# A two-block model on one core: small vectors moved to other queues, the first norm scaled by rows and turned by plain transposes, the first weight chunk split in halves

## The chip, the core and the metric

The kernel runs on one core of a Trainium2 chip, as one launch. The metric is the device time of that launch in microseconds (us), taken as the median of several executions. Everything is float32; large products are made of three fp32r products (below).

## The reference

Two transformer-like blocks follow one another on x of 256 tokens by 1024 features. Only the start matters here: the first layer of the first block is a Conformer convolution.

```python
def rmsnorm(x, g):
    xf = x.astype(jnp.float32)
    y = xf * lax.rsqrt(jnp.mean(xf * xf, axis=-1, keepdims=True) + EPS)
    return (y * g.astype(jnp.float32)).astype(x.dtype)

def conformer_conv(x, norm_g, pw1_w, pw1_b, dw_w, dw_b, ln_g, ln_b, pw2_w, pw2_b):
    a, b = jnp.split(rmsnorm(x, norm_g) @ pw1_w + pw1_b, 2, axis=-1)      # 1024 -> 2 x 1024
    h = a * jax.nn.sigmoid(b)
    h = lax.conv_general_dilated(h, dw_w[:, None, :], ...) + dw_b         # 31 causal taps, by channel
    h = jax.nn.silu(layernorm(h, ln_g, ln_b))
    return h @ pw2_w + pw2_b
```

What follows is a gated FFN, an attention with compressed, selected and windowed keys, a second FFN, a final norm, and then the second block (projections, mLSTM and forgetting attention, cross attention, an FFN, the last norm).

## The kernel before

**Work and buffers.** Every weight matrix is cut into chunks of up to 128 x 2048 values (1 MB). SP loads chunk c into `raw[c % 4]` (RAWS = 4) once the chunk four before it has been split; ScalarE (ACT) rounds it to `split_hi` (L579, a copy to fp32r), VectorE (DVE) writes the rest as `split_lo` (L944), and TensorE (PE) makes each product from three (L1469 to L1471). For five chunks of the start (numbers 3 and 6 of the first projection, and the first three of the second) GpSimd (POOL) writes `split_lo` instead (L544, list `by_pool`). There is no planner: each engine has its program written out in order, and semaphores join them. So an instruction that waits holds up all that stands behind it on its engine.

**The order of the start.** SP issues the two halves of x (`h`), chunk 0, five small vectors (L480), then the six loads of taps (L482: `taps` is 31 rows of 4 KB plus 4 rows of 4 KB, `pos` four small blocks), and then chunks 1, 2 and so on. ACT issues six small vectors (L572) and POOL three (L499). All 14 vectors lie as 128 rows in `vecs`; PE turns them at once (L1568) and DVE copies them to `vecT` (L986), from which gains and biases are then read as columns.

**The first norm.** ACT squares and sums each of the two token tiles (L597), POOL makes the reciprocal root (L506, L509), ACT puts it on a diagonal (`root_diag`, L592), and PE multiplies x by that diagonal, which turns and scales it in one step (`turn`, L1484: 16 products of 128 x 128, each of them two MATMULs in the trace). ACT writes the high half `xn_hi` of the turned, gained values (`take_hi`, L617, four pairs), DVE the low half `xn_lo` (`take`, L963).

**The first projection and the convolution.** `pw1` has eight chunks, one for each feature tile ft. For ft = 0 PE goes through the eight slices kt of the input as `xn_lo` comes; after ft = 0 it turns the taps (`turn_taps`, L1576 and L1579, which wait for `taps_loaded`), and then goes on with ft = 1 to 7. For every ft, ACT first splits chunks up to ft + 2, then takes the sigmoid (L647), and builds diagonals of taps (L637) after DVE has copied the taps (L1004, L1007); DVE splits up to ft + 2, then makes the gated value `u` (L996). After ft = 1, DVE starts its share of the 31 taps (L1025 for the first, L1028 for the others), with the remaining splits and gates put in after every four taps. PE does the other channels' taps (L1599).

Of the kernel before, what the change touches and what calls it, by code (L numbers as in the profile page):

```python
# [67 lines left out]
def build_kernel(nc, a, out):  # L68
# [8 lines left out]
    with ctx:  # L77
# [121 lines left out]
        vecs_loaded_pool = sem("vecs_loaded_pool")  # L199
        vecs_loaded_sp = sem("vecs_loaded_sp")  # L200
        small_loaded = sem("small_loaded")
# [256 lines left out]
        for b, name in enumerate(("cmp_pos_k", "cmp_pos_v")):  # L458
            for g in range(2):
                tap_loads.append((pos[:, P * b + DH * g:P * b + DH * g + DH], a[name]))  # L460
        pool_loads, act_loads, sp_loads = vec_loads[0:3], vec_loads[3:9], vec_loads[9:]


        @block.sync
        def _(sp):
# [3 lines left out]
            for c, parts in enumerate(chunks):  # L469
                if c >= RAWS:  # L470
                    last = c - RAWS
                    if is_split[last]:
                        sp.wait_ge(*lo_count(last))
                    else:
                        sp.wait_ge(*freed[last])
                for place, src in parts:
                    sp.dma_start(place(raw[c % RAWS]), src).then_inc(raw_loaded[c % RAWS], 16)  # L477
                if c == 0:
                    for dst, src in sp_loads:
                        sp.dma_start(dst, src).then_inc(vecs_loaded_sp, 16)  # L480
                    for dst, src in tap_loads:
                        sp.dma_start(dst, src).then_inc(taps_loaded, 16)  # L482
# [87 lines left out]
        def _(sc):  # L570
            for dst, src in act_loads:
                sc.dma_start(dst, src).then_inc(vecs_loaded, 16)  # L572
            def split(c, m):

                sc.wait_ge(raw_loaded[c % RAWS], loads_through(c))
                if m >= SPLITS:
                    sc.wait_ge(*freed[of_split[m - SPLITS]])
                n = used_cols[c]
                nc.scalar.activation(split_slot[m % SPLITS][0][:, 0:n], raw[c % RAWS][:, 0:n],  # L579
                                     ACT.Copy).then_inc(split_hi, 1)  # L580

            through = splitter(split)

            def squares(k, src, ready, together=False):

                idx = turning.index(k) if k in turning else None

                def diagonal(t):
                    if idx:
                        sc.wait_ge(turned, 4 * idx)  # L590
                    sc.wait_ge(rstd_ready, TT * k + t + 1)
# [3 lines left out]
                for t in range(TT):  # L595
                    ready(t)
                    nc.scalar.activation(scaled[:, t, :], src[:, t, :], ACT.Square, scale=D ** -0.5,  # L597
                                         accum_out=ssq[:, TT * k + t:TT * k + t + 1]).then_inc(ss_ready, 1)
                    if idx is not None and not together:
                        diagonal(t)  # L600
                for t in range(TT if together else 0):
                    diagonal(t)

# [4 lines left out]

            def take_hi(k, which=0):

                name, off = gains[k][which]
                for n in range(4):
                    if which == 0:
# [319 lines left out]
        def _(ve):  # L933
# [12 lines left out]
            def split(c, m):  # L946
# [3 lines left out]
                ve.wait_ge(split_hi, m + 1)  # L950
                n, (hi, lo) = used_cols[c], split_slot[m % SPLITS]
                less_hi(lo[:, 0:n], raw[c % RAWS][:, 0:n], hi[:, 0:n]).then_inc(split_lo, 1)

            through = splitter(split)

            def take(k, which=0):

                name, off = gains[k][which]
                for n in range(4):
                    ve.wait_ge(xn_hi, xn_before[k] + 4 * which + n + 1)  # L960
# [486 lines left out]
        def _(te):  # L1447
# [4 lines left out]
            def weights(stage, n, k, unsplit=False):  # L1452
# [7 lines left out]
                te.wait_ge(*lo_count(c))  # L1460
                return c, [kn(s, used_cols[c] // k, k) for s in split_slot[nth[c] % SPLITS]]
# [16 lines left out]
            def turn(k, src=h):  # L1478

                idx = turning.index(k)  # L1480
                for t in range(TT):
                    te.wait_ge(root_diag_ready, TT * idx + t + 1)
                    for kt in range(KT):
                        x = mm(bank[kt // 2][:, S * (kt % 2) + P * t:S * (kt % 2) + P * t + P],  # L1484
                               src[:, t, P * kt:P * kt + P], root_diag[:, t, :], start=True, stop=True)
                        if t == TT - 1 and kt % 2:
                            x.then_inc(turned, 1)

            def features(dst, w, c0, ready=None):
# [18 lines left out]
            def feature_pair(stage, n, b, before=None, ready=None):  # L1508
# [4 lines left out]
                for j in range(2):  # L1513
                    x = features(bank[b][:, S * j:S * j + S], w, P * j, ready if j == 0 else None)
                used(c, x)
# [50 lines left out]
            te.wait_ge(vecs_loaded_pool, 16 * len(pool_loads))  # L1566
            te.wait_ge(vecs_loaded_sp, 16 * len(sp_loads))
            nc.tensor.transpose(bank[4][:, 0:P], vecs, ident[:, :]).then_inc(pre_turned, 1)  # L1568
# [373 lines left out]
```

## Time and profile before

| | |
|---|---|
| median of 3 runs | 1200.13 us (1198.3 to 1204.06) |
| the profiled execution | 1200.32 us, its span 1198.5 us |
| busy of the span: PE, PEld, DVE, ACT, POOL | 94%, 83%, 56%, 46%, 8% |
| first 31.7 us: PE, DVE, ACT busy | 20.3, 12.4, 18.6 us |
| 31.7 to 120.5 us: PE, DVE, POOL busy | 77.5, 88.8, 25.0 us |
| mean granted PE clock | 0.956 of full |

PE is TensorE's products and PEld its weight loads, which overlap them. The span runs from the first instruction to the last; the profiled execution was 1.8 us longer than its span. The time of a stage is not read from the busy shares but from what the engine that ends the stage waited for. In the rows, times are microseconds from the start of the span; "x8" is the number of instructions merged into a line; the bracket at the end of a line is the idle time before it and what ended it; "SPq" and "ACTq" are the queues in which SP and ACT issue transfers.

### The profile page before, as it was taken

What the parts mean: (1) busy time and instruction counts of PE and PEld (TensorE: products, weight loads), DVE (VectorE), ACT (ScalarE), POOL (GpSimd) and SP (SyncE); (2) the same over time, 40 slices, a digit from 0 to 9 for tenths busy, and PEclk for the clock granted to TensorE, in tenths of its full rate; (3) what the DMA queues carried; (4) which work ended last, traced back from release to release, by engine and by line L of the source; (5) the groups of instructions that cost most, each with busy time, mean ns of one, the idle gap of its engine ahead of it and who ended that gap; (6) DMA issues with size and microseconds to landing.
All of it is one profiled execution on the core that took longest, in us unless ns stands there. A gap on an engine that the chain in (4) does not pass through costs nothing.

```text
span 1198.5 us, 17458 instructions
## 1 busy us (share of the span) xinstructions
PE 1122.6 (94%) x7303; PEld 996.4 (83%) x7303; DVE 674.5 (56%) x1099; ACT 549.7 (46%) x888; POOL 92.2 (8%) x107
## 2 busy tenths in 40 slices
PE   6996699999999988899999979999999999999997
PEld 6985479999989955689999979999756888999996
DVE  3999545455455379555544547546424445555554
ACT  5760344444443478454444345535423444444442
POOL 3440056000010000000000010000000000000000
PEclk9998699999999889899999989999958999999999
DMA  8650045666582600546667554554402424655640
GB/s 234 197 150 1 3 139 176 195 183 185 177 182 71 236 11 1 171 137 197 182 177 207 178 159 140 168 186 141 141 1 71 141 72 145 205 177 176 209 142 35
DMA packets 188312, 170.74 MB, mean 142 GB/s; under 512 B 15398, under 2 KB 164006, under 8 KB 188234
## 3 DMA queue, kind: packets, MB, share of 16 engines
q1 hardware_dynamic: 187128, 167.20, 45.8%
q10 hardware_dynamic: 1010, 2.43, 0.6%
q8 instruction: 57, 0.93, 0.3%
q14 instruction: 21, 0.17, 0.0%
q0 software_dynamic: 96, 0.02, 0.0%
HBM read 168.58 MB, written 1.05 MB: 142 GB/s over the span
## 4 chain that ended last, share of the span: by engine, by line
PE 79%; DVE 14%; ACT 3%; POOL 1%; SPq 1%; issue 1%; DMA 1%; POOLq 0%; ACTq 0%; DVEq 0%
PE bank L1469 23%; PE bank L1470 23%; PE bank L1471 23%; DVE v L1028 6%; PE bank L1484 1%; PE bank L1818 1%; PE bank L1817 1%; ACT scaled L597 1%; DVE soft L1165 1%; DVE split_lo L944 1%; DVE soft L1146 1%; PE bank L1645 1%; SPq L477 1%; PE bank L1841 1%; POOL msq L506 1%
## 5 line engine op out<-in xcount | busy, mean ns | idle before, releaser
L944 DVE TENSOR_TENSOR split_lo<-raw,split_hi 128x2048 fp32r<-128x2048 f32 (+1 forms) x152 | 344.5, 2268 | 244.5 <-ACT split_hi L579 244.5
L1469 PE MATMUL bank<-xn_hi,split_hi 128*128 128x256 f32 x1440 | 410.9, 285 | 3.7 <-DVE xn_lo L963 3.6
L1470 PE MATMUL bank<-xn_lo,split_hi 128*128 128x256 f32 x1440 | 408.4, 284 | 0.0
L1471 PE MATMUL bank<-xn_hi,split_lo 128*128 128x256 f32 x1440 | 408.3, 284 | 0.0
L579 ACT ACTIVATE split_hi<-raw 128x2048 fp32r<-128x2048 f32 (+1 forms) x157 | 296.5, 1890 | 151.3 <-PE bank L1471 145.2
L1469 PEld LDWEIGHTS bank<-xn_hi,split_hi 128*128 128x128 f32 x1440 | 277.1, 192 | 7.6 <-issue 5.5
L1470 PEld LDWEIGHTS bank<-xn_lo,split_hi 128*128 128x128 f32 x1440 | 277.2, 193 | 1.3
L1471 PEld LDWEIGHTS bank<-xn_hi,split_lo 128*128 128x128 f32 x1440 | 277.2, 192 | 0.0
L1469 PE MATMUL bank<-split_hi,ffa_hi 128*128 128x512 f32 x304 | 118.7, 390 | 0.0
L1470 PE MATMUL bank<-split_lo,ffa_hi 128*128 128x512 f32 x304 | 118.7, 390 | 0.0
L1471 PE MATMUL bank<-split_hi,ffa_lo 128*128 128x512 f32 x304 | 118.3, 389 | 0.0
L1469 PE MATMUL bank<-split_hi,xn_hi 128*128 128x512 f32 (+3 forms) x256 | 96.5, 377 | 5.1 <-DVE xn_lo L944 5.1
L1470 PE MATMUL bank<-split_lo,xn_hi 128*128 128x512 f32 (+3 forms) x256 | 95.4, 373 | 0.0
L1471 PE MATMUL bank<-split_hi,xn_lo 128*128 128x512 f32 (+3 forms) x256 | 95.3, 373 | 0.0
L695 ACT ACTIVATE soft<-bank 128x256 f32<-128x256 f32 x44 | 16.9, 385 | 137.0 <-PE bank L1471 137.0
L1028 DVE SCALAR_TENSOR_TENSOR v<-u,tapT,v 128x256 f32<-128x256 f32 x147 | 75.3, 580 | 0.0
L506 POOL TENSOR_SCALAR msq<-ssq 128x1 f32<-128x1 f32 x20 | 10.6, 528 | 755.8 <-ACT scaled L597 755.5
L1471 PEld LDWEIGHTS bank<-split_hi,ffa_lo 128*128 128x128 f32 x304 | 57.1, 188 | 12.0
L1469 PEld LDWEIGHTS bank<-split_hi,ffa_hi 128*128 128x128 f32 x304 | 57.2, 188 | 11.0
L1470 PEld LDWEIGHTS bank<-split_lo,ffa_hi 128*128 128x128 f32 x304 | 57.2, 188 | 10.6
L1469 PEld LDWEIGHTS bank<-split_hi,xn_hi 128*128 128x128 f32 x256 | 49.8, 194 | 17.5 <-DVE xn_lo L944 5.0
L1471 PEld LDWEIGHTS bank<-split_hi,xn_lo 128*128 128x128 f32 x256 | 49.7, 194 | 8.4
(256 smaller groups left out, 1103.2 us busy)
## 6 DMA issues: line engine op xcount, KB each, us to landing
raw<-in_ffn_w_in SPq DMA_DIRECT2D x88, 512.0 KB, 5.2
raw<-in_w_ff SPq DMA_DIRECT2D x32, 1024.0 KB, 5.1
raw<-in_ffn_w_out SPq DMA_DIRECT2D x22, 1024.0 KB, 4.8
raw<-in_w_in SPq DMA_DIRECT2D x14, 1024.0 KB, 5.5
raw<-in_a_pw_w SPq DMA_DIRECT2D x16, 512.0 KB, 6.9
raw<-in_w_xkv SPq DMA_DIRECT2D x8, 1024.0 KB, 5.3
raw<-in_a_pw_w SPq DMA_DIRECT2D x4, 1024.0 KB, 5.4
raw<-in_b_w_in SPq DMA_DIRECT2D x4, 1024.0 KB, 6.1
```

What stands on the lines that cost most here:

```text
L477: sp.dma_start(place(raw[c % RAWS]), src).then_inc(raw_loaded[c % RAWS], 16)
L506: nc.gpsimd.tensor_scalar(msq[:, c:c + 1], ssq[:, c:c + 1], EPS, None, ALU.add).then_inc(ms_ready, 1)
L579: nc.scalar.activation(split_slot[m % SPLITS][0][:, 0:n], raw[c % RAWS][:, 0:n], ACT.Copy).then_inc(split_hi, 1)
L597: nc.scalar.activation(scaled[:, t, :], src[:, t, :], ACT.Square, scale=D ** -0.5, accum_out=ssq[:, TT * k + t:TT * k + t + 1]).then_inc(s ...
L695: nc.scalar.activation(softf[:, b], bank[ft % 4][:, 0:S], ACT.Silu).then_inc(gate_act, 1)
L944: return nc.vector.tensor_tensor(dst, src, hi.bitcast(F32), ALU.subtract)
L1028: x = nc.vector.scalar_tensor_tensor(out=dst, in0=src, scalar=tap, in1=dst, op0=ALU.mult, op1=ALU.add)
L1146: x = nc.vector.tensor_tensor_reduce(out=scores_of(i)[:, piece], in0=src, in1=bias, scale=-DH ** -0.5, scalar=3e38, op0=ALU.add, op1=ALU.m ...
L1165: x = nc.vector.tensor_scalar(scores_of(i)[:, piece], scores_of(i)[:, piece], coef[:, i % 2, n:n + 1], None, ALU.mult)
L1469: mm(dst, left[0], right[0], start=start, stop=False)
L1470: mm(dst, left[0], right[1], start=False, stop=False)
L1471: return mm(dst, left[1], right[0], start=False, stop=stop)
```

## The change

The five small vectors leave SP: ACT now issues the first twelve of the 14, POOL the last two. The six loads of taps go behind chunk 3 instead of behind chunk 0. The first norm no longer builds diagonals on ACT: DVE multiplies the rows of each token tile by their reciprocal root into `scaled`, and PE turns `scaled` with 16 plain transposes. Chunk 0 is split in two halves of 1024 columns: ACT writes the first high half, then the first two pairs of `xn_hi`, then the second half, then the other two pairs; DVE does the same with the low halves; PE starts ft = 0 after the first low half and waits for the second at kt = 4. All other norms keep their diagonals.

```diff
-        pool_loads, act_loads, sp_loads = vec_loads[0:3], vec_loads[3:9], vec_loads[9:]
+        pool_loads, act_loads = vec_loads[12:], vec_loads[0:12]
...
-                if c == 0:
-                    for dst, src in sp_loads:
-                        sp.dma_start(dst, src).then_inc(vecs_loaded_sp, 16)
+                if c == RAWS - 1:
                     for dst, src in tap_loads:
                         sp.dma_start(dst, src).then_inc(taps_loaded, 16)
...
-                n = used_cols[c]
-                nc.scalar.activation(split_slot[m % SPLITS][0][:, 0:n], raw[c % RAWS][:, 0:n],
+                n, done = used_cols[c], 0
+                if c == 0:
+                    done = SLOT // 2
+                    nc.scalar.activation(split_slot[0][0][:, 0:done], raw[0][:, 0:done],
+                                         ACT.Copy).then_inc(first_hi, 1)
+                    sc.wait_ge(pre_copied, 1)
+                    take_hi(CONV, ns=range(2))
+                nc.scalar.activation(split_slot[m % SPLITS][0][:, done:n], raw[c % RAWS][:, done:n],
                                      ACT.Copy).then_inc(split_hi, 1)
...
-            squares(CONV, h, lambda t: sc.wait_ge(x_loaded[t], 16), together=True)
+            squares(CONV, h, lambda t: sc.wait_ge(x_loaded[t], 16))
             through(0)
-            sc.wait_ge(pre_copied, 1)
-            take_hi(CONV)
+            take_hi(CONV, ns=range(2, 4))
...
             ve.wait_ge(pre_copied, 1)
+            for t in range(TT):
+                ve.wait_ge(rstd_ready, t + 1)
+                nc.vector.tensor_scalar(scaled[:, t, :], h[:, t, :], rstd[:, t:t + 1], None,
+                                        ALU.mult).then_inc(x_scaled, 1)
+            ve.wait_ge(first_hi, 1)
+            half = slice(0, SLOT // 2)
+            less_hi(split_slot[0][1][:, half], raw[0][:, half], split_slot[0][0][:, half]).then_inc(first_lo, 1)
+            take(CONV, ns=range(2))
             through(0)
-            take(CONV)
+            take(CONV, ns=range(2, 4))
...
-                    te.wait_ge(root_diag_ready, TT * idx + t + 1)
+                    te.wait_ge(*((root_diag_ready, TT * (idx - 1) + t + 1) if idx else (x_scaled, t + 1)))
                     for kt in range(KT):
...
+                        if idx:
+                            x = mm(dst, src[:, t, P * kt:P * kt + P], root_diag[:, t, :], start=True, stop=True)
+                        else:
+                            x = nc.tensor.transpose(dst, scaled[:, t, P * kt:P * kt + P], ident[:, :])
...
                 for kt in range(KT):
+                    if rest and kt == KT // 2:
+                        te.wait_ge(*rest)
```

## Rows read from the trace of the kernel before

**Rows 1.** The page's chain of work that ended last, shares of the span.
```profile
PE 79%; DVE 14%; ACT 3%; POOL 1%; SPq 1%; issue 1%; DMA 1%; POOLq 0%; ACTq 0%; DVEq 0%
```

**Rows 2.** The same chain in order of time, start: start us, us, what.
```profile
16.04 6.69 DMA raw<-in_a_pw_w
...
22.75 1.92 ACT split_hi L579
...
31.09 0.49 DVE u L996
```

**Rows 3.** The timeline of the first 24.5 us: start us, us, engine, line, operation.
```profile
2.79 0.35 ACTq L572 DMA_DIRECT2D pt<-in_final_norm  x1
...
4.54 1.28 ACT L597 ACT_TABLE_LOAD   x1 [4.54 <-DMA h<-in_x]
...
8.41 0.58 POOL L509 TENSOR_TENSOR rstd<-msq,nhalf 128x1 f32<-128x1 f32 x1
...
10.82 0.45 PE L1568 MATMUL bank<-ident,pt 128*128 128x128 f32 x1 [10.82 <-DMA pt<-in_ln]
...
15.63 3.03 ACT L617 ACTIVATE xn_hi<-bank,vecT 128x256 fp32r<-128x256 f32 x8 [4.18 <-PE bank L1484]
...
17.53 0.36 PE L1469 MATMUL bank<-xn_hi,split_hi 128*128 128x256 f32 x1 [0.61 <-DVE xn_lo L963]
...
23.57 0.69 PE L1576 MATMUL bank<-ident,v 35*128 35x35 f32 x8
```

**Rows 4.** Transfer packets by size, of 9.0 to 15.5 and of 15.5 to 16.9 us.
```profile
DMA packets 2134, 1.14 MB, mean 176 GB/s; under 512 B 202, under 2 KB 2099, under 8 KB 2134
...
DMA packets 143, 0.07 MB, mean 48 GB/s; under 512 B 16, under 2 KB 143, under 8 KB 143
```

**Rows 5.** Stretches: start:end, length; last: PE clock, mean share of 16 transfer engines, GB/s.
```profile
16.00:16.50 0.50, 0.50 (x7) 0.50 (x6) 0.00 (x0) 0.50 (x3) 0.00 (x0) 1.00 0.08 23
...
26.00:30.00 4.00, 4.00 (x35) 4.00 (x35) 1.87 (x4) 2.55 (x5) 0.00 (x0) 1.00 1.15 293
```

**Rows 6.** Transfers by line: count, KB each, median us from issue to landing.
```profile
out<-scaled SPq DMA_DIRECT2D x2, 512.0 KB, 2.6
...
pt<-in_a_norm POOLq DMA_DIRECT2D x1, 4.0 KB, 5.8
```

**Rows 7.** DVE's instruction groups by shape: count, busy us, mean ns, idle before.
```profile
L944 DVE TENSOR_TENSOR split_lo<-raw,split_hi 128x2048 fp32r<-128x2048 f32 x150 | 343.7, 2293 | 242.6 <-ACT split_hi L579 242.6
...
L1165 DVE TENSOR_SCALAR soft<-soft,coef 128x256 f32<-128x256 f32 x24 | 7.3, 346 | 0.0
...
L1165 DVE TENSOR_SCALAR soft<-soft,coef 128x128 f32<-128x128 f32 x24 | 5.7, 280 | 0.0
```

**Rows 8.** PE: the first turn (min/median/max ns), and eight plain transposes later on.
```profile
L1484 PE MATMUL bank<-root_diag,h x32: 274/421/421, 11.1 to 16.6; 128*128 128x128 f32 x32
...
911.17 0.86 PEld L1857 LDWEIGHTS bank<-ident,u 128*128 128x128 f32 x8 [0.17 <-issue]
```

**Rows 9.** The timeline of POOL and DVE during the taps, 30 to 57 us.
```profile
30.78 4.63 POOL L544 TENSOR_TENSOR split_lo<-raw,split_hi 128x2048 fp32r<-128x2048 f32 x1 [15.76 <-ACT split_hi L579]
...
46.69 6.80 POOL L544 TENSOR_TENSOR split_lo<-raw,split_hi 128x2048 fp32r<-128x2048 f32 x1 [11.28 <-ACT split_hi L579]
...
31.68 4.21 DVE L1025 TENSOR_SCALAR v<-u,tapT,vecT 128x256 f32<-128x256 f32 x2
...
45.75 3.24 DVE L1028 SCALAR_TENSOR_TENSOR v<-u,tapT,v 128x256 f32<-128x256 f32 x8
...
49.31 7.23 DVE L1028 SCALAR_TENSOR_TENSOR v<-u,tapT,v 128x256 f32<-128x256 f32 x8
```

**Rows 10.** Stretches later: length; busy us of PE, PEld, DVE, ACT, POOL; PE clock.
```profile
31.70:120.50 88.80, 77.46 (x481) 71.42 (x480) 88.80 (x162) 43.88 (x107) 25.03 (x5) 0.95 0.38 112
...
110.00:112.00 2.00, 0.00 (x0) 0.00 (x0) 2.00 (x6) 0.00 (x0) 0.00 (x0) 0.77 0.00 0
...
433.00:436.00 3.00, 3.00 (x17) 1.41 (x14) 1.39 (x7) 2.01 (x10) 0.00 (x0) 0.50 0.00 0
```

More of the change, by code:

```diff
@@ L199, in build_kernel @@
         vecs_loaded_pool = sem("vecs_loaded_pool")
-        vecs_loaded_sp = sem("vecs_loaded_sp")
+        first_hi = sem("first_hi")
+        first_lo = sem("first_lo")
+        x_scaled = sem("x_scaled")
         small_loaded = sem("small_loaded")
@@ L577, in split, with squares @@
                     sc.wait_ge(*freed[of_split[m - SPLITS]])
-                n = used_cols[c]
-                nc.scalar.activation(split_slot[m % SPLITS][0][:, 0:n], raw[c % RAWS][:, 0:n],
+                n, done = used_cols[c], 0
[6 more added lines that the diff above has]
+                nc.scalar.activation(split_slot[m % SPLITS][0][:, done:n], raw[c % RAWS][:, done:n],
                                      ACT.Copy).then_inc(split_hi, 1)
             through = splitter(split)
-            def squares(k, src, ready, together=False):
+            def squares(k, src, ready):
                 idx = turning.index(k) if k in turning else None
                 def diagonal(t):
-                    if idx:
-                        sc.wait_ge(turned, 4 * idx)
+                    sc.wait_ge(turned, 4 * idx)
                     sc.wait_ge(rstd_ready, TT * k + t + 1)
@@ L598, in squares @@
                                          accum_out=ssq[:, TT * k + t:TT * k + t + 1]).then_inc(ss_ready, 1)
-                    if idx is not None and not together:
+                    if idx:
                         diagonal(t)
-                for t in range(TT if together else 0):
-                    diagonal(t)
             def h_squares(k):
@@ L607, in h_squares, with take_hi @@
                 squares(k, h, lambda t: sc.wait_ge(h_ready, h_count(k, t)))
-            def take_hi(k, which=0):
+            def take_hi(k, which=0, ns=range(4)):
                 name, off = gains[k][which]
-                for n in range(4):
+                for n in ns:
                     if which == 0:
@@ L951, in split, with take @@
                 n, (hi, lo) = used_cols[c], split_slot[m % SPLITS]
+                if c == 0:
+                    less_hi(lo[:, n // 2:n], raw[0][:, n // 2:n], hi[:, n // 2:n]).then_inc(split_lo, 1)
+                    return
                 less_hi(lo[:, 0:n], raw[c % RAWS][:, 0:n], hi[:, 0:n]).then_inc(split_lo, 1)
             through = splitter(split)
-            def take(k, which=0):
+            def take(k, which=0, ns=range(4)):
                 name, off = gains[k][which]
-                for n in range(4):
+                for n in ns:
                     ve.wait_ge(xn_hi, xn_before[k] + 4 * which + n + 1)
@@ L1459, in weights @@
                     return c, raw[c % RAWS]
-                te.wait_ge(*lo_count(c))
+                te.wait_ge(*((first_lo, 1) if c == 0 else lo_count(c)))
                 return c, [kn(s, used_cols[c] // k, k) for s in split_slot[nth[c] % SPLITS]]
@@ L1513, in feature_pair @@
                 for j in range(2):
-                    x = features(bank[b][:, S * j:S * j + S], w, P * j, ready if j == 0 else None)
+                    x = features(bank[b][:, S * j:S * j + S], w, P * j, ready if j == 0 else None,
+                                 lo_count(0) if c == j == 0 else None)
                 used(c, x)
```

7 lines of the change are left out of this document (3 added, 4 removed).

## The prediction

> **What bounds the kernel now.** I read the page's chain of waits first. It is TensorE for 79% and DVE for 14% [rows 1]; in the stretch from 31.7 to 120.5 us DVE is busy for all of its 88.8 us, PE for 77.5 [rows 10]. So two things can end the start: DVE's convolution taps, which follow on its second gated value at 31.09 us [rows 2], and PE's eight feature tiles, which feed them. Whatever the change brings has to show as an earlier start of that stretch; behind it everything runs relative to it. The whole start before the taps is 31 us, and 0.5% of the kernel, about what a measurement of it can tell from no change, is 6.0 us. That alone makes a large result unlikely.
>
> Then I followed what leads to 31.09. The chain in order of time goes from chunk 2's transfer, issued at 16.04 and landed 6.69 us later, over its split on ACT at 22.75 and DVE's half of it to the gated values [rows 2]. PE's own line runs beside it: the vectors land at 10.82, ACT begins `take_hi` at 15.63 after 4.18 us of idling, PE begins ft = 0 at 17.53, turns the taps at 23.57, and goes on with ft = 1 behind them [rows 3]. ft = 0 took 5.9 us, to 23.4; ft = 1, begun near 24.4 behind 0.9 us of turning, ends near 30.3, and with ACT's sigmoid of 0.5 us behind it that is 0.3 us ahead of 31.09. Both lines are therefore nearly critical, and the later of the two decides after the change.
>
> **The vectors.** ACT's six loads end at 3.14, each 0.35 us [rows 3]; six more make it 5.2. x landed at 4.54 [rows 3], so the squares start 0.7 us later, and the second reciprocal root, which was done at 8.99 [rows 3], comes at 9.65. For the landing of the last vector the nearest rows are 2.6 us (an unhurried store) and 5.8 us (POOL's vector among the same traffic) [rows 6]: 7.8 to 11.0 us. I take 9.2, nearer to the loaded row's middle. The last one landed at 10.82 before. PE turns them in 0.45 us [rows 3], and with 0.3 for DVE's copy `vecT` stands at 10.0 in place of 11.6.
>
> **The scaling.** A DVE multiply by a column costs 280 ns at 128 columns and 346 at 256 [rows 7], 66 ns per 128, so 742 ns at 1024: two take 1.5 us, with 0.3 for POOL, which builds masks then. The first tile is ready at 10.9, the second at 11.8. ACT saves its two diagonals (off the path now, since it idles 4.18 us behind them [rows 3]).
>
> **The transposes.** The old turn is 32 MATMULs, mostly at 421 ns and at 274 in the end [rows 8], from 11.06; ACT got its first pair after about 20 of them, 4.5 us. Now PE makes 16, and the first pair needs ten. Eight plain ones took 0.86 us at full rate [rows 8]; double that for an engine just out of idling, 0.2 each: 2.0 us. ACT begins `take_hi` at about 13.0 instead of 15.63, 2.6 us earlier.
>
> **The halves.** The first chunk was split at no cost before, while ACT and DVE had nothing else to do. The first half still is free. The second (0.95 us on ACT, half of 1.92 [rows 2], and 1.15 us on DVE, half of 2.29 [rows 7]) now stands between the second and the third pair of `xn`. From 15.63 to PE's first product were 1.9 us [rows 3], so PE starts at 14.9; it would want kt = 4 at 16.4, but ACT writes two pairs to 14.5, the half to 15.5, the third pair to 16.2, and DVE its half to 16.7 and the third pair to 17.6. PE waits 1.2 us there, and ends ft = 0 at 22.2 against 23.4. So of the 2.6 us the halving gives back 1.2 to 1.4. As far as PE's line goes, the change is worth 1.2 us, with the vectors at their bounds 2.6 or a loss of 0.6.
>
> **The taps' loads.** This is what I expect to decide. They were behind chunk 0 on SP's queue and are now behind chunk 3, and PE must turn them between ft = 0 and ft = 1. Between 9.0 and 15.5 us exactly 35 packets of 2 KB and more went through, none after that [rows 4]: these are the 31 + 4 rows of 4 KB of `taps`, so they took 6 us and more, about one row in 0.18 us. At 16.0 to 16.5 the 16 transfer engines were busy for 0.08 at 23 GB/s [rows 5]: a single engine, still behind with its share of chunk 1, with the other 15 out of work. The rows of taps thus go one behind the other through one engine, at some 21 GB/s. That also explains chunk 1's late landing before, and it means that moving the loads frees chunks 1 to 3: at 293 GB/s [rows 5] a chunk takes 3.6 us, and with chunk 0 through at 9.0, where the large packets began, they land near 12.5, 16 and 19.5 (on that one engine 64 KB at 20 GB/s are 3.3 us, so its third share ends at 18.9); ACT and DVE no longer wait for chunks 1 and 2. But the taps start at 18.9, need 5.4 us (their 124 KB at 23 GB/s) to 6.4, and a landing adds about 0.9: they are there at 25.2 to 26.2, I take 25.7. PE ended ft = 0 at 22.2: it idles 3.5 us, turns the taps till 26.6, and starts ft = 1 2.2 us later than the 24.4 of before.
>
> The Trainium skill says why one engine: in "DMA: Bandwidth & Descriptors", section "Why a DMA increments its semaphore by 16 and not by 1", a hardware-issued transfer runs on the largest count up to 16 that divides its slowest dimension on both sides, and 31 rows leave 1. The packets of [rows 4] agree with it; by the page's 27 GiB/s for an engine 124 KB would be 4.4 us, an estimate that would land the taps near 24.2.
>
> **From there to the taps' arithmetic.** `tapT` is copied by 26.9, ACT's first diagonals end at 28.1 and chunk 3's high half at 30.0, POOL's low half runs 30.0 to 34.6 (4.63 us [rows 9]). The sigmoid of ft = 1 waits for PE until 32.5, `u` is there at 33.4 instead of 31.5. And yet DVE loses nothing by that: its first two taps, of a shape that costs 0.35 us each [rows 7], took 4.21 us before, the first until 35.6, just to the end of POOL's 30.78 to 35.41, and eight taps took 7.23 us instead of 3.24 beside POOL's next one [rows 9]. DVE's taps and POOL's subtraction exclude each other. After the change DVE idles through most of POOL's piece, and is through its first tap at about 34.9 against 35.56. Its later gates wait for PE's tiles, 2.1 us later than before: 1.5 us for the fifth tile's, in part while POOL runs anyway. I put the end of the taps between 0 and 1.6 us later, and take 0.8.
>
> **The sum.** +0.7 (ACT's issue) is inside the 9.65 and hidden behind the vectors; PE line -1.2, taps' landing +3.4 on PE, together +2.2 at ft = 1; of these, 1.4 is swallowed by POOL's piece: +0.8. The profiled execution of 1200.32 would be 1201.1, the median of 1200.13 gives 1200.9. Behind 120.5 no instruction changes, only the phase of PE's clock, for which I have no price but the 1.5 us to either side that the three runs lie apart.
>
> **Rivals.**
> The taps are in time (landed by 22.2: the engine's rows go faster than 18.8 + 3.4, or turn out to be spread). Then PE's line counts, -1.2, and POOL's piece, starting before DVE is ready, adds up to 2 us: 1196.9 to 1199, about 1197.8. For it: nothing in the old trace waits for the taps, so their landing is never seen; against: the 35 packets in 6 us.
>
> PE's clock. With PE idle its granted clock fell from full towards half within 110 to 112 [rows 10], and at the start it took most of the first turn's 5.9 us until MATMULs came down from 421 to 274 ns [rows 8]. An idle stretch of 3.5 us ahead of ft = 1 can do the same: some 4 us of work at half rate cost 2 us more on PE, and DVE's gates follow: +2.5 to +4, 1203.4. The Trainium skill, "TensorE: Matmul & The Clock Gate", section "Part 4: PE-mode transpose", states that transposes do not count as work for the clock; if so, the first norm no longer warms PE for ft = 0, which by the half rate above would cost up to 2 us there, mostly hidden by the wait for the taps. The trace does not contradict: at 433 to 436, among attention's transposes, PE is busy throughout at clock 0.50 [rows 10].
>
> Slower than the measure can miss: the same wait for the taps, if the landing is at 31.5 us or later (each us later than 26 is a full us on PE and, past POOL's piece, on DVE). It would take the taps' engine another 5 us, as if chunk 4's traffic slowed it to half. The median would be 1206 and more. Against it: the taps shared the engines with chunk 1 before, and took 6.4 us.
>
> The change does not do what it says, since the vectors still land near 11 us: PE's ft = 0 ends at 24.0, still before the taps: the time is the same as in the forecast.
>
> **How the numbers follow.** Taps late, with the forecast's small loss (vectors late or not): 0.50. Taps in time: 0.31, of which 0.04 reach 1194.1. Clock: 0.14, of which 0.01 reaches 1206.1. Taps very late: 0.05. That is 0.04 faster by over 0.5%, 0.90 within, 0.06 slower. The range reaches over the case of taps in time and that of the clock, 1196.5 to 1204.5; the likeliest case's own is 1199 to 1203.
>
> **What would show it.** Right: the 35 large packets lie at about 19 to 25 us, PE's L1576 starts near 25.7 with an idle stretch of some 3 us ended by a transfer; `take_hi` starts at 13.0, PE's first product at 14.9, with a gap of about 1 us at kt = 4; chunk 2 is split without a wait for its transfer; POOL's L544 starts near 30 while DVE idles, and the first L1025 ends near 35. Wrong: L1576 directly behind ft = 0 (rival one), MATMULs of ft = 1 mostly at the slow duration (rival two). The step that I trust least is the landing of the taps, then how DVE, POOL and PE share the next 40 us.

## The result and the profile after

The changed kernel takes 1205.8 us (median of 9 runs, 1204.63 to 1207.61), the kernel before 1200.33 beside it (9 runs, 1198.3 to 1204.06): ratio 1.0045, 95% interval 1.0032 to 1.0058. That is 5.5 us slower, outside the range of the prediction (1196.5 to 1204.5) and 0.45% where the prediction had set the line of a slower kernel at 0.5%.

| | before | after |
|---|---|---|
| span of the profiled execution | 1198.5 | 1204.1 us |
| vectors landed (PE turns them) | 10.82 | 10.95 |
| first `take_hi` on ACT | 15.63 | 15.06 |
| PE's first product of ft = 0 | 17.53 | 16.95 |
| PE done with ft = 0 (end of its last product) | 23.64 | 24.98 |
| PE turns the taps | 23.57 | 28.11 |
| end of DVE's taps (start of the line that adds PE's) | 120.49 | 125.76 |

The last line is the measure that I use below: up to it the taps are 5.27 us late, and the span is 5.6 us longer. So the loss is made in the start and only carried from there. It also is a sharper measure than the total time, as the section on the experiments shows.

The page's chain of the kernel after, shares of the span, answers to [rows 1]: PE has 2% more, DVE 2% and ACT 1% less.

```profile
PE 81%; DVE 12%; ACT 2%; SPq 1%; POOL 1%; issue 1%; DMA 1%; POOLq 0%; ACTq 0%; DVEq 0%
```

The same chain in order of time, for [rows 2]. It no longer goes through chunk 2, its split and the gated value, but through the last of the taps' loads and then PE:

```profile
15.49 1.69 SPq L482
17.23 0.79 SPq L482
...
19.34 8.72 DMA pt<-in_cmp_pos_v
28.11 1.06 PE bank L1594 x8
...
29.52 0.51 PE bank L1482
30.03 0.21 PE bank L1483
...
35.48 0.12 PE bank L1483
```

Two things are to be seen. The transfer issued at 19.34 is complete 8.72 us later, and PE's products behind it are 0.21 us apart until 35 us, 0.12 from there on. The timeline of the start, for [rows 3]:

```profile
5.31 0.33 ACTq L572 DMA_DIRECT2D pt<-in_ln_x  x1
5.73 1.28 ACT L602 ACT_TABLE_LOAD   x1 [5.73 <-issue]
...
9.60 0.58 POOL L509 TENSOR_TENSOR rstd<-msq,nhalf 128x1 f32<-128x1 f32 x1
...
10.95 0.45 PE L1586 MATMUL bank<-ident,pt 128*128 128x128 f32 x1 [10.95 <-DMA pt<-in_ln_x]
...
11.76 1.45 DVE L995 TENSOR_SCALAR scaled<-h,rstd 128x1024 f32<-128x1024 f32 x2
...
12.56 3.67 PE L1501 MATMUL bank<-ident,scaled 128*128 128x128 f32 x16 [1.17 <-DVE scaled L995]
...
15.06 1.57 ACT L620 ACTIVATE xn_hi<-bank,vecT 128x256 fp32r<-128x256 f32 x4 [4.07 <-PE bank L1501]
...
16.95 0.55 PE L1482 MATMUL bank<-xn_hi,split_hi 128*128 128x256 f32 x1 [0.71 <-DVE xn_lo L968]
...
18.87 3.76 ACT L585 ACTIVATE split_hi<-raw 128x2048 fp32r<-128x2048 f32 x2
...
28.11 1.06 PE L1594 MATMUL bank<-ident,v 35*128 35x35 f32 x8 [3.13 <-DMA pt<-in_cmp_pos_v]
```

The twelve vectors on ACT's queue are issued by 5.64 and land at 10.95: nothing is won on the 10.82 of before. Chunks 1 and 2 are split back to back (18.87, no idle time ahead), so they do come earlier. And PE idles 3.13 us for the taps. The granted clock of the stretches around that wait (length; busy us of PE, PEld, DVE, ACT, POOL; clock; share of the transfer engines; GB/s), for [rows 10]:

```profile
25.00:27.00 2.00, 0.00 (x0) 0.00 (x0) 0.84 (x2) 0.47 (x1) 0.00 (x0) 1.00 0.74 217
27.00:29.00 2.00, 0.90 (x8) 0.90 (x8) 0.00 (x0) 0.00 (x0) 0.00 (x0) 0.78 0.38 110
29.00:31.00 2.00, 2.00 (x11) 1.86 (x11) 0.58 (x2) 1.18 (x4) 0.00 (x0) 0.50 0.80 222
31.00:33.00 2.00, 2.00 (x11) 2.00 (x11) 0.00 (x0) 1.60 (x1) 0.31 (x1) 0.50 0.91 268
33.00:35.00 2.00, 2.00 (x12) 2.00 (x11) 0.00 (x0) 0.00 (x0) 2.00 (x1) 0.51 1.09 314
35.00:37.00 2.00, 2.00 (x19) 2.00 (x19) 0.00 (x0) 0.00 (x0) 2.00 (x1) 1.00 0.62 174
```

PE is busy throughout from 29 on, with 11 products in 2 us at clock 0.50 (the 1.2 GHz level) and 19 at 1.00 (2.4 GHz). ft = 1 takes from 29.5 to 37.6 us, 8.2 instead of 5.9 of before. The packets of the stretches 16 to 20 and 20 to 28 us, for [rows 4], show where the taps were:

```profile
DMA packets 2176, 1.08 MB, mean 270 GB/s; under 512 B 90, under 2 KB 2175, under 8 KB 2176
...
DMA packets 2203, 1.18 MB, mean 148 GB/s; under 512 B 178, under 2 KB 2169, under 8 KB 2203
```

One large packet before 20 us and 34 from there to 28, with the mean rate down to 148 GB/s from 270. The beginning of the taps on DVE and POOL, for [rows 9]:

```profile
32.69 4.58 POOL L544 TENSOR_TENSOR split_lo<-raw,split_hi 128x2048 fp32r<-128x2048 f32 x1 [16.73 <-ACT split_hi L585]
...
38.42 0.48 DVE L1009 SCALAR_TENSOR_TENSOR u<-bank,vecT,soft 128x256 f32<-128x256 f32 x1 [8.63 <-ACT soft L649]
39.00 0.74 DVE L1038 TENSOR_SCALAR v<-u,tapT,vecT 128x256 f32<-128x256 f32 x2
...
125.76 0.42 DVE L1052 TENSOR_TENSOR v<-v,bank 128x256 f32<-128x256 f32 x1
```

POOL's piece is over at 37.27, before DVE has its gated value, and the first two taps take 0.74 us in place of 4.21.

### The profile page after: what moved, and what is told of

Read it like the earlier page. It is cut to its first block, busy times and chain, and to the rows that moved or that the text cites. A ratio compares the mean times of both kernels' runs of the same rounds, so it can differ in the third digit from the quotient of the medians.

```text
span 1204.1 us, 17428 instructions
## 1 busy us (share of the span) xinstructions
PE 1125.5 (93%) x7287; PEld 998.8 (83%) x7287; DVE 671.9 (56%) x1102; ACT 548.8 (46%) x887; POOL 88.9 (7%) x106
## 4 chain that ended last, share of the span: by engine, by line
PE 81%; DVE 12%; ACT 2%; SPq 1%; POOL 1%; issue 1%; DMA 1%; POOLq 0%; ACTq 0%; DVEq 0%
PE bank L1482 24%; PE bank L1483 24%; PE bank L1484 24%; DVE v L1041 5%; PE bank L1499 1%; PE bank L1836 1%; PE bank L1835 1%; SPq L479 1%; ACT scaled L602 1%; DVE soft L1178 1%; DVE soft L1159 1%; DMA pt<-in_cmp_pos_v 1%; PE bank L1663 1%; PE bank L1859 1%; POOL msq L506 1%
## 5 line engine op out<-in xcount | busy, mean ns | idle before, releaser
L585 ACT ACTIVATE split_hi<-raw 128x2048 fp32r<-128x2048 f32 (+2 forms) x157 | 295.6, 1885 | 147.9 <-PE bank L1484 145.4
L697 ACT ACTIVATE soft<-bank 128x256 f32<-128x256 f32 x44 | 16.9, 385 | 137.0 <-PE bank L1484 137.0
```

The source lines that it names most:

```text
L585: nc.scalar.activation(split_slot[m % SPLITS][0][:, done:n], raw[c % RAWS][:, done:n], ACT.Copy).then_inc(split_hi, 1)
L697: nc.scalar.activation(softf[:, b], bank[ft % 4][:, 0:S], ACT.Silu).then_inc(gate_act, 1)
```

## The experiments

All of them in one table. "Taps' end" is the start of DVE's L1039 of before, under whatever line number; "rest" is the span less that time; "clock" is PE's granted clock in 420 to 500 us, in attention.

| run | median us | ratio to before, 95% | first product | taps turned | taps' end | rest | clock |
|---|---|---|---|---|---|---|---|
| before | 1200.33 | | 17.53 | 23.57 | 120.49 | 1078.0 | 0.91 |
| after | 1205.8 | 1.0045 (1.0032 to 1.0058) | 16.95 | 28.11 | 125.76 | 1078.3 | 0.91 |
| e1_taps_back | 1201.73 | 1.0016 (0.9997 to 1.0034) | 17.60 | 24.89 | 120.52 | 1075.9 | 0.94 |
| e2_taps_only | 1205.6 | 1.0051 (1.0033 to 1.0070) | 17.46 | 28.02 | 124.65 | 1081.5 | 0.89 |
| e3_taps_16_15 | 1200.43 | 0.9998 (0.9978 to 1.0018) | 17.12 | 24.40 | 119.13 | 1081.4 | 0.87 |
| e4_fill | 1202.2 | 1.0019 (0.9999 to 1.0040) | 16.91 | 27.97 | 122.70 | 1073.9 | 0.94 |
| e5_no_halves | 1200.11 | 0.9997 (0.9981 to 1.0014) | 16.77 | 23.14 | 117.89 | 1080.9 | 0.91 |
| e6_before_16_15 | 1196.72 | 0.9988 (0.9970 to 1.0005) | 17.14 | 23.17 | 118.14 | 1075.7 | 0.94 |
| e7_sp_vecs_first | 1199.91 | 1.0003 (0.9986 to 1.0020) | 16.41 | 23.83 | 118.59 | 1079.5 | 0.87 |
| e8_diag_vecs_first | 1200.87 | 1.0011 (0.9995 to 1.0027) | 16.26 | 23.58 | 118.33 | 1080.8 | 0.91 |
| e9_combined | 1197.82 | 0.9987 (0.9972 to 1.0001) | 15.09 | 22.27 | 117.53 | 1076.0 | 0.94 |
| e10_vecs_only | 1200.92 | 1.0003 (0.9988 to 1.0017) | 17.50 | 23.54 | 120.35 | 1078.8 | 0.87 |
| e11_scaling_only | 1200.49 | 1.0004 (0.9989 to 1.0019) | 17.59 | 25.65 | 120.40 | 1078.0 | 0.91 |
| e12_before_16_15_again | 1198.93 | 0.9999 (0.9980 to 1.0017) | 17.49 | 23.54 | 118.43 | 1075.8 | 0.94 |

The column "rest" covers code that no edit touches, and yet lies between 1073.9 and 1081.5. The five profiles with 1076.0 and less are the five with that clock at 0.94; all others have 0.91 or less. So a start that is 2 us shorter can't be read from one total, and hardly from a median. The taps' end tells it better (118.14 and 118.43 for e6 and e12, which are the same kernel), but each run has one profile, and PE's clock within the start moves that end too: by 1 to 2 us in after, e7 and e11, as said at each.

### e1: the taps' loads back behind chunk 0

```diff
-                if c == RAWS - 1:
+                if c == 0:
                     for dst, src in tap_loads:
```

> The changed kernel with one edit undone: the loads of the taps stand behind chunk 0 again. If their late landing is the loss (PE idle 3.1 us before the taps, ft = 1 begun at 29.5 instead of 24.4 and at half clock until 34.9), PE turns the taps directly behind ft = 0, ft = 1 begins near 25.8 at full clock, and the time falls by 4 to 6 us against the changed kernel, to 1200 to 1202. If the vectors, the halves or the plain transposes are the loss, at least 3 of the 5.5 us stay: 1203.5 or more.

PE turned the taps without a wait at 24.89 and the taps' end came back to 120.52, all of the loss. ACT, by its line of chunk 2, waits for the chunks again, as before:

```profile
22.79 1.92 ACT L585 ACTIVATE split_hi<-raw 128x2048 fp32r<-128x2048 f32 x1 [1.19 <-DMA raw<-in_a_pw_w]
```

The move of the loads is what costs; the other parts together are worth nothing (120.52 against 120.49).

### e2: that move alone, in the kernel before

```diff
                         sp.dma_start(dst, src).then_inc(vecs_loaded_sp, 16)
+                if c == RAWS - 1:
                     for dst, src in tap_loads:
```

> The kernel before with one edit: the loads of the taps go behind chunk 3. If the taps' landing is the loss, PE ends ft = 0 near 23.4 and still waits until about 28, and the time is 1204.5 to 1206.5, the whole of the loss from this edit alone. If the rest of the change carries the loss, it stays within 2 us of 1200.3.

In the median it makes the whole loss by itself (ratio 1.0051), and PE waits as in this line:

```profile
28.02 1.06 PE L1577 MATMUL bank<-ident,v 35*128 35x35 f32 x8 [4.45 <-DMA pt<-in_cmp_pos_v]
```

At the taps' end it makes 4.2 of the 5.3 us (124.65 against 125.76 of after). The taps landed at the same time, so the missing 1.1 us are not theirs. The granted clock stood at half by 27 us already, while PE idled (0.50 in 27 to 29), and was back at full by 33, two us sooner than in after. Two us at half rate are one of work. The windows (columns as above):

```profile
30.00:32.00 2.00, 2.00 (x11) 2.00 (x11) 0.00 (x0) 2.00 (x4) 0.00 (x0) 0.50 0.90 248
32.00:34.00 2.00, 2.00 (x16) 2.00 (x15) 0.00 (x0) 0.53 (x1) 1.39 (x1) 0.85 0.99 272
```

### e3: the same place, but the 31 rows in two loads of 16 and 15

```diff
-        tap_loads.append((taps[0:TAPS, :], a["a_dw_w"][0]))
+        tap_loads.append((taps[0:16, :], a["a_dw_w"][0][0:16, :]))
+        tap_loads.append((taps[16:TAPS, :], a["a_dw_w"][0][16:TAPS, :]))
```

> The changed kernel with the 31 rows of taps loaded as 16 rows and 15 rows. If the rows went one behind the other through one transfer engine, the two loads spread over many engines, the taps land 4 to 6 us earlier (22 to 24 instead of 28.1), PE waits for them not at all or under 1 us, and the time is 1199 to 1202. If the landing is late for another reason (the queue's order, the small position loads, the traffic as a whole), it stays near 28 and the time at 1205 or more.

PE's line has no wait left in it, at the same place in SP's queue:

```profile
24.40 0.69 PE L1595 MATMUL bank<-ident,v 35*128 35x35 f32 x8
```

The taps' end is 119.13, 6.63 us ahead of after and 1.36 ahead of before. So it was not the place in the queue by itself, but the one transfer engine on which 31 rows go. The rule of the Trainium skill that the prediction used ("DMA: Bandwidth & Descriptors", section "Why a DMA increments its semaphore by 16 and not by 1") is borne out as far as the packets show it: 16 of the 35 large ones went through before 20 us and the other 19 before 24, where in after 14 of them came only after 24, and the load that was complete at 28.1 us is no longer waited for at 24.4. It is in time only just, though: where PE was done with ft = 0 sooner, it waited at this place even for 16 and 15 rows, 0.25 us in e5 (until 23.14) and 1.20 us in e8 (until 23.58).

### e4: PE kept busy while it waits

```diff
                 if ft == 0:
+                    for _ in range(8):
+                        mm(bank[7][:, 0:S], ident[:, :], h[:, 0, 0:S], start=True, stop=True)
                     turn_taps()
```

> The changed kernel with eight idle products of PE (identity by 256 columns of x, into a bank that nobody reads) put between ft = 0 and the wait for the taps. The wait stays. If the clock that falls in it costs about 2 us on PE, ft = 1 runs at full clock, ends near 35.5 instead of 37.6, and the time falls by 1 to 2 us, to 1204. If the clock costs nothing in the end, because DVE's taps are held up by POOL's subtraction anyway, it stays within 0.5 us of 1205.8.

Eight products that nobody reads fill the wait (16 MATMULs), and the taps land as late as before:

```profile
24.11 3.62 PE L1605 MATMUL bank<-h,ident 128*128 128x256 f32 x16
27.97 0.69 PE L1594 MATMUL bank<-ident,v 35*128 35x35 f32 x8 [0.24 <-DMA pt<-in_cmp_pos_v]
```

The windows of the same run, columns as above, beside those of after: 18 and 19 products in 2 us in place of 11.

```profile
29.00:31.00 2.00, 2.00 (x18) 2.00 (x19) 0.28 (x2) 1.69 (x4) 0.00 (x0) 1.00 0.85 217
31.00:33.00 2.00, 2.00 (x19) 2.00 (x19) 0.00 (x0) 1.11 (x1) 0.81 (x1) 1.00 1.06 301
```

Useless work on PE makes the taps' end 3.06 us earlier than in after (122.70 against 125.76) and 1.95 us earlier than in e2, and the median 3.6 and 3.4 us less: 1202.2, where 1204 was expected. That is the price of the clock alone, 2 to 3 us at the taps' end by how long it stayed low after PE had begun again; 2.21 us over before is the price of the late landing without it. (The ratios' intervals overlap a little, by 0.0008 with that of after; the taps' end is the firmer of the two readings.)

### e5: e3 without the halves

```diff
-                if c == 0:
-                    done = SLOT // 2
-                    nc.scalar.activation(split_slot[0][0][:, 0:done], raw[0][:, 0:done],
-                                         ACT.Copy).then_inc(first_hi, 1)
-                    sc.wait_ge(pre_copied, 1)
-                    take_hi(CONV, ns=range(2))
...
             through(0)
-            take_hi(CONV, ns=range(2, 4))
+            sc.wait_ge(pre_copied, 1)
+            take_hi(CONV)
```

(DVE's halves and PE's waits go with them.)

> The changed kernel with the taps loaded as 16 and 15 rows, and with chunk 0 split in one piece again (ACT splits it whole before the first pair of xn, DVE whole before its first pair). Beside the run with the halves kept (taps 16 and 15: PE's first product at 17.1, ft = 0 over at 24.3, conv taps over near 119.2). If the halving costs, as its second half stands between the second and the third pair, PE starts at 17.1 to 17.6 but runs ft = 0 without the gap and ends it at 23.0 to 23.5, 0.8 to 1.3 us earlier, and the taps' arithmetic ends near 118.2. If the halving pays, ft = 0 ends later than 24.3.

ACT splits the whole of chunk 0 while it has nothing else to do, and `take_hi` is one run of eight:

```profile
10.10 1.91 ACT L580 ACTIVATE split_hi<-raw 128x2048 fp32r<-128x2048 f32 x1 [0.84 <-DMA raw<-in_a_pw_w]
14.87 3.03 ACT L615 ACTIVATE xn_hi<-bank,vecT 128x256 fp32r<-128x256 f32 x8 [2.86 <-PE bank L1490]
```

ft = 0 takes 6.1 us (16.77 to 22.9) instead of 7.4 (17.12 to 24.5), and the taps' end is 1.24 us earlier, 117.89. The halving is a loss as long as the vectors and not the chunk come last.

### e6 and e12: the kernel before with 16 and 15 rows, and nothing else

The edit is that of e3, made in the kernel before, where the loads stand behind chunk 0. It was run twice.

> The kernel before, with only the 31 rows of taps loaded as 16 and 15 rows, at their old place behind chunk 0. If one transfer engine was kept back by the rows, no stretch is left with only one engine at work, chunks 1 and 2 land 3 to 5 us earlier (before: 19.4 and 22.7), and ACT no longer waits for them. The end of DVE's taps hardly moves, since PE's ft = 1 (over at 30.3) is then what the second gate waits for: 119.5 to 120.5 against 120.5; the time is 1199 to 1200.5. If chunk 2's landing was what set the old start, the gain is 1.5 us and more.

> The kernel before with only the taps as 16 and 15 rows, once more (1196.72 before, ratio 0.9988), on one chip with the other candidate. Its start ended 2.35 us earlier than that of before; the ratio should come out at 0.998, within its interval of about 0.0017, so 1197 to 1199. If the earlier median owed its extra microsecond to the clock of later stages, this one is nearer to 1198.5.

The taps' end is 118.14 and 118.43, 2.1 to 2.4 us ahead of before, where the first expectation had 119.5 to 120.5. ACT now splits chunks 1 and 2 without a wait (18.11 in e6, the same line that in [rows 2] waited for chunk 2's transfer until 22.75):

```profile
18.11 3.77 ACT L580 ACTIVATE split_hi<-raw 128x2048 fp32r<-128x2048 f32 x2
```

But that is not yet the gain: the second gated value waits for PE's ft = 1 all the same, and comes only 0.1 us (e12) to 0.5 us (e6) earlier than the 31.09 of before. The rest comes through POOL. It gets chunk 3 two us earlier and is done with it two us earlier, so DVE's first two taps beside it take 2.33 us in place of 4.21 [rows 9]. In e12, DVE and then POOL:

```profile
30.95 0.48 DVE L997 SCALAR_TENSOR_TENSOR u<-bank,vecT,soft 128x256 f32<-128x256 f32 x1 [5.11 <-ACT soft L648]
31.53 2.33 DVE L1026 TENSOR_SCALAR v<-u,tapT,vecT 128x256 f32<-128x256 f32 x2
...
28.75 4.63 POOL L545 TENSOR_TENSOR split_lo<-raw,split_hi 128x2048 fp32r<-128x2048 f32 x1 [13.75 <-ACT split_hi L580]
```

0.14 and 1.88 us make 2.02 of the 2.06. By its size that is the expectation's second case (1.5 us and more), but what set the old start was not chunk 2's landing by way of the gated value; the late chunks cost by way of POOL's subtraction.

Ratios 0.9988 and 0.9999 (0.998 was expected of the second): neither interval is clear of 1.

### e7 and e8: five vectors ahead of chunk 0

SP's five vectors are issued between x and chunk 0; e7 does this in e5, e8 in the kernel before, with the taps in 16 and 15 rows behind chunk 3 in both. The vectors stand on three queues again in e7 (ACT six, POOL three, SP five), as in before.

```diff
+            for dst, src in sp_loads:
+                sp.dma_start(dst, src).then_inc(vecs_loaded_sp, 16)
             for c, parts in enumerate(chunks):
```

> The changed kernel with taps in 16 and 15 rows, chunk 0 in one piece, and the vectors on three queues as before the change (ACT six, POOL three, SP five), SP's five between x and chunk 0. The last vector landed at 10.9 to 11.6 with twelve on ACT's queue. If ACT's packets were the late ones, held back by the weights' packets beside them, the last vector lands at 8.5 to 9.5, PE's first product comes at 15.5 to 16.5, ft = 0 ends near 22, and the taps' arithmetic near 117: 1197.5 to 1199. If the vectors are late by the load on the engines as such, they still land at 10.5 or later and nothing moves.

> The kernel before (diagonals, chunk 0 in one piece) with SP's five vectors between x and chunk 0, and the taps in 16 and 15 rows behind chunk 3. Against the run beside it, which differs by scaling rows on DVE and plain transposes, it prices that part alone: the vectors should land at the same 8.5 to 9.5, PE's turn of 32 MATMULs starts at 9.1 to 9.5 and ends near 15, its first product comes near 16. If the plain transposes pay (16 instead of 32), this one starts its first product 0.5 us later or more; if the wait for DVE's scaling eats that up, it starts earlier.

The vectors are in at 8.58 and 8.45 us, 2.1 us and more earlier than in any run that has them behind chunk 0 or on ACT's queue. But chunk 0 comes later by about 1 us, and now it is what is waited for, as e7's ACT and PE show:

```profile
11.18 1.91 ACT L583 ACTIVATE split_hi<-raw 128x2048 fp32r<-128x2048 f32 x1 [3.38 <-DMA raw<-in_a_pw_w]
...
16.41 0.36 PE L1474 MATMUL bank<-xn_hi,split_hi 128*128 128x256 f32 x1 [2.32 <-DVE xn_lo L964]
```

The first product is only 0.4 us earlier than in e5 (e7), or 0.9 us than in e6 (e8), and the taps' end is no earlier (118.59 and 118.33, where 117 was expected of e7). In neither run is chunk 0 the whole reason. In e7 ft = 0 takes 7.5 us (16.41 to 23.9) instead of the 6.1 of e5: behind PE's wait of 2.32 us the granted clock fell, to 0.80 in 17.4 to 18 us and 0.50 from 18 to 21, and products took 0.41 us until 21.0. In e8 ft = 0 ran at full rate and was over at 22.4, but then PE waited for the taps:

```profile
23.58 0.69 PE L1577 MATMUL bank<-ident,v 35*128 35x35 f32 x8 [1.20 <-DMA pt<-in_cmp_pos_v]
```

e8 was also to price the plain transposes. Beside e7 its first product is 0.15 us earlier (16.26 against 16.41), so where chunk 0 is late they win nothing.

### e9: what the runs had spoken for, together

The kernel after with the five vectors first, the halves kept, the taps as 16 and 15 rows behind chunk 0.

> The changed kernel (scaled rows, plain transposes, halves) with the vectors on three queues, SP's five ahead of chunk 0, and the taps as 16 and 15 rows behind chunk 0. With the vectors in at 8.5 and chunk 0 later (11.2, as in the run with one piece), chunk 0 is what the first product waits for, and there the halving should pay: first product near 14.5 to 15, ft = 0 over at 21.4 to 22.5, the taps' arithmetic over near 116.5, 1.5 us before any other run. If the halving costs here as well, ft = 0 ends at 23 or later and the taps' arithmetic at 118.5.

With chunk 0 as what is late, the halves bring the first product 1.3 us earlier than in e7 (15.09 for 16.41), and PE gives 1.03 us back at kt = 4. ft = 0 is over at 22.3; e7 at full rate would have been there at 22.5, an estimate from its first product and the 6.1 us of e5. So here the halves cost nothing, but a gain of theirs beyond 0.2 us is not shown. ACT's first half and PE's first product:

```profile
11.82 1.06 ACT L585 ACTIVATE split_hi<-raw 128x1024 fp32r<-128x1024 f32 x1 [3.91 <-DMA raw<-in_a_pw_w]
...
15.09 0.35 PE L1486 MATMUL bank<-xn_hi,split_hi 128*128 128x256 f32 x1 [0.92 <-DVE xn_lo L972]
```

The first product is 2.4 us earlier than before, the taps' end, 117.53, 2.96 us (116.5 was expected). The median is 1197.82 and the ratio 0.9987 (0.9972 to 1.0001): the best start of all, and a gain that the total does not show beyond its interval. It is clearly better than after, not clearly better than before.

### e10 and e11: the vectors alone, and the scaling alone

e10 moves only the vectors, in the kernel before:

```diff
-        pool_loads, act_loads, sp_loads = vec_loads[0:3], vec_loads[3:9], vec_loads[9:]
+        pool_loads, act_loads = vec_loads[12:], vec_loads[0:12]
```

> The kernel before with one edit: the vectors as in the change (ACT twelve, POOL two, none on SP); the taps stay whole behind chunk 0. If moving the vectors brings them no sooner (10.95 after, 10.82 before), PE's first product stays at 17.3 to 18.3 and the taps' arithmetic ends at 120.3 to 121.2. If it had helped by itself, the vectors land at 9.5 or earlier.

```profile
10.85 0.45 PE L1564 MATMUL bank<-ident,pt 128*128 128x128 f32 x1 [10.85 <-DMA pt<-in_ln_x]
```

Nothing moves: 10.85 against 10.82, taps' end 120.35 against 120.49. e11 is e6 with the scaled rows and the plain transposes of the change.

> The kernel before with the taps as 16 and 15 rows behind chunk 0, and the first norm as in the change (rows scaled on DVE, plain transposes), nothing else. Beside the run with only the taps in two pieces (vectors 11.2, first product 17.1, taps' arithmetic over at 118.1) it prices the norm's part. By the durations (16 transposes of 0.23 us against 32 MATMULs in 5.05 to 5.9, less DVE's scaling ahead of them) the first product comes 0 to 0.7 us earlier, and so does the end at 118.1; a loss would put it at 118.5 or later.

```profile
17.59 0.55 PE L1474 MATMUL bank<-xn_hi,split_hi 128*128 128x256 f32 x1 [0.71 <-DVE xn_lo L964]
18.37 0.41 PE L1474 MATMUL bank<-xn_hi,split_hi 128*128 128x256 f32 x1
```

Its vectors were not turned before 11.56 us, later than in all other runs but e1, and the 16 transposes took 3.67 us; the first product is at 17.59 and each takes 0.41 us until 22.4, the duration that products have where the granted clock reads 0.50. The expectation had the first product 0 to 0.7 us earlier than in e6; it is 0.4 us later. The taps' end is 120.40, 2.0 to 2.3 us behind e6 and e12, for which the slow ft = 0 (8.1 us, 17.59 to 25.7, against 6.1 in e12) is enough. Whether that slow clock comes with the scaling is not settled: see below.

## Why the prediction was wrong

**Right: the mechanism.** The taps' loads decide, they go through one transfer engine, they are late for PE, and their last one ends an idle stretch of some 3 us (3.13; forecast 3.5). e2 alone makes the loss (in the median all of it, at the taps' end 4.2 of 5.3 us) and e3 alone removes it. Chunk 2 is split without a wait, as forecast, and POOL's piece runs while DVE idles, though at 32.69 and not near 30, and the first of DVE's taps ends at 39.4, not near 35. The up to 2 us that the first rival put on POOL's piece starting sooner are there as well: 1.9 us in e6 and e12.

**The step that failed: leaving PE's clock out of the sum.** The prediction saw an idle stretch of 3.5 us ahead of ft = 1, and treated the clock as a rival with 0.14. In the profile of after the clock was 0.78 in 27 to 29 and 0.50 until 35 us; in e2 it was 0.50 in 27 to 31 and full from 33. e4, which keeps it full, prices it at 2.0 us (against e2) to 3.1 us (against after) at the taps' end, and its median of 1202.2 lies inside the range. The rival's own price, 2 us on PE, was near: ft = 1 took 2.3 us longer (8.2 for 5.9) and the turn of the taps 0.4 us. But its sum, 1203.4, had the early landing in it.

**The term that was mis-sized: the landing.** Forecast 25.7, measured 28.11 (28.02 in e2). I let the engine begin at 18.9, give the taps all its rate, and added 0.9 us for a landing, which no row showed (in after PE began some 0.2 us after the lone engine's traffic ended, near 27.9). It began at 20 (one large packet before), and needed 8 us for 34 rows. In 26.5 to 27.9 us it works alone at last, as the GB/s of 40 slices of this stretch show:

```profile
GB/s 59 73 161 88 44 88 51 103 30 44 37 15 29 15 29 15 29 15 29 15 29 15 29 15 29 15 29 15 29 15 29 15 29 15 29 15 29 15 29 15
```

That is about 22 GB/s; at that rate 8 us would carry 176 KB, and the 34 rows are 136. The rest would be its share of the chunks around the taps. That is argued from these numbers, and no run separates it.

**The sum by its terms.** Late landing without the clock: +2.2 us at the taps' end (e4), forecast +0.8. Clock: +3.1, forecast 0. Together +5.3, and the median rose by 5.5. On PE the landing alone put ft = 1 off by 4.4 us (28.82 in e4 for 24.42), twice the forecast 2.2. What POOL's piece was to swallow, 1.4 us, was too small as well: by e4 it is 2.2. DVE's rows give both sums. In e4 the second gated value is 4.3 us late (35.38 for 31.09), the first two taps take 1.32 us for 4.21, and DVE then waits 0.66 us for a split of ACT: 2.1 of the 2.2 us. In after these are 7.3 us (38.42), 0.74 us and 1.25 us: 5.1 of the 5.3.

**PE's line, -1.2 us, was wrong as well, though hidden by the wait.** ft = 0 ended at 24.98, not at 22.2. The vectors landed at 10.95, not at 9.2; that is the fourth rival, and e10 shows it alone. Everything behind is 1.4 to 2.1 us late by that: scaled tiles (the second at 13.2 for 11.8), transposes (0.23 us each, forecast 0.2), `take_hi` at 15.06 for 13.0, first product at 16.95 for 14.9. The halves cost what I said: without them 1.24 us are won (e5), and in e1, e3 and e4 PE waits 1.14 us at kt = 4 (forecast 1.2). The line of e4:

```profile
19.72 0.36 PE L1482 MATMUL bank<-xn_hi,split_hi 128*128 128x256 f32 x1 [1.14 <-DVE xn_lo L968]
```

After itself has no such wait, since its products took 0.41 us until 21.2 and filled it; its ft = 0 ends 0.7 us later than that of e4 (24.98 against 24.3), which the wait for the taps hides.

**The transposes and the clock.** The old turn kept PE busy from 11.1 to 16.6 [rows 8], and in all six profiles that have it (before, e2, e6, e8, e10, e12) ft = 0 ran at full rate, in e8 behind a wait of 1.95 us. Behind the new transposes PE began at full rate in e1, e3, e4, e5, e7 and e9 (first product 0.36 us, later ones 0.28), of which e7 fell to half 1.3 us later, and at half in after and e11 (0.55, then 0.41). Two lines of the windows from 17.7 to 21 us, of after and then of e4:

```profile
17.70:21.00 3.30, 3.30 (x17) 3.12 (x16) 2.83 (x6) 3.30 (x6) 0.00 (x0) 1.00 0.81 197
```

```profile
17.70:21.00 3.30, 2.16 (x19) 1.98 (x18) 2.83 (x6) 3.30 (x6) 0.00 (x0) 1.00 0.81 199
```

After is busy for all of the 3.3 us with fewer products than e4 makes in 2.2. The clock column reads 1.00 in both; here only the durations show the rate. The statement of the Trainium skill ("TensorE: Matmul & The Clock Gate", section "Part 4: PE-mode transpose"), that transposes don't count as work for the clock, would have half rate in the first product of all eight runs, and six contradict it (the page's durations are for bf16, these transposes are float32). Up to 21 us after and e4 have the same instructions at nearly the same times and got different rates, so the scaled form leaves the rate to chance here; what decides it stays open. The prediction's support for that statement from 433 to 436 us of before was misread: until 435.93 PE ran attention's score products there (L1655 to L1661), and it had idled 2.7 us before 430.92.

**The chances.** The clock (0.14) and the very late taps (0.05) were priced each by itself. But a late landing and the clock are no alternatives: the second followed from the first. It did behind the waits of 3.13 us (after) and 4.45 us (e2); behind the waits of 1.14 us in e3 and 1.20 us in e8 the clock stayed at 1.00. Split as if they were, each ended inside or near the range, and their sum, 1205.8, outside.

## What to carry to other kernels

Before a load is moved later in a queue, look at its number of rows: 31 rows went through one transfer engine, and PE got the last of that group 12.6 us after its issue began; the same bytes as 16 and 15 rows were there 4.5 to 5 us sooner at the same place, in time or up to 1.2 us late. A wait that you put on PE can cost more than its own length, by the clock behind it: where the profile shows a clock below full after an idle stretch, put it in the sum and not among the rivals (here 2 to 3 us behind waits of 3.1 and 4.5 us). And take a stage's end from a profile (here the taps' end, 118.14 and 118.43 for the same kernel) when the rest of the kernel moves the total by more than the edit is worth, and look at the durations of PE's products on the way there, since a low clock moves that end as well.

## What the runs showed of the hardware that I had not expected

A load on one transfer engine delays what stands behind it in the queue too. In the kernel before this cost 2.1 to 2.4 us at the taps' end without any wait for the taps themselves (e6 and e12). At 16.0 to 16.5 us of before 23 GB/s went through [rows 5], about what the lone engine moves in the GB/s shown above, while ACT still waited for chunk 1, until 19.43.

Small loads that were issued earlier on a second queue, beside the chunks, were not complete earlier. The last of the vectors was issued by 7.19 us on SP's queue in before and by 5.64 on ACT's in after, and landed at 10.82 and 10.95; in the other versions with twelve on ACT's queue it was 10.76 to 11.58. With SP's five ahead of chunk 0, all 14 were issued by 3.7 and in by 8.64, and chunk 0 came about 1 us later in exchange. Whether the place ahead of the chunk or the earlier issue brings this, no run separates.

With the same instructions behind the start, the granted clock of 420 to 500 us lay between 0.87 and 0.94 from profile to profile, and the rest of the span between 1073.9 and 1081.5 us. What sets it was not found.
